# The start of a hybrid attention layer: zeros through TensorE, half of the copies on ScalarE, one chain of roots for four blocks

## The reference

```python
h = rms_norm(x, g_pre)            # x * rsqrt(mean(x*x) + eps) * g
proj = h @ w_in                   # 1024 x 7424, split in 11 parts
ya = short_gated_conv(...) * silu(a_z)
q, k = partial_rope(b_q), partial_rope(b_k)
yb = window_attention_with_sink(q, k, b_v, sink) * silu(b_z)
ym = memory_cross_attention(m_q, mk, mv) * silu(m_z)
merged = g0 * (ya @ w_up_a) + g1 * (yb @ w_up_b) + g2 * (ym @ w_up_m)
out = x + rms_norm(merged @ w_out, g_post)
```

## Time and profile before

| | us |
|---|---|
| runs | 942.90, 941.89, 942.04; median 942.04 |
| profiled execution | 942.66 |
| its span, first to last instruction | 940.8 |
| TensorE busy in the span | 915.8 (97%) |
| VectorE, ScalarE, GpSimd busy | 619.5, 422.6, 378.4 |

### The profile page before, as it was taken

How to read it: one execution, slowest core, us unless ns; L and a number is a source line. 1 busy time by engine, 2 the same in 40 slices (tenths; PEclk the granted TensorE clock), 3 DMA queues, 4 the chain that set the end, 5 groups by cost and what they waited for, 6 DMA issues and landing times. The chain is left out here.

```text
span 940.8 us, 12512 instructions
## 1 busy us (share of the span) xinstructions
PE 915.8 (97%) x4360; PEld 768.4 (82%) x4360; DVE 619.5 (66%) x1057; ACT 422.6 (45%) x802; POOL 378.4 (40%) x260
## 2 busy tenths in 40 slices
PE   5999999999999999999999999999999999999997
PEld 4788778888888888888888888888888888888885
DVE  5799966655556666656576278888896367763443
ACT  7434465444445466544462434343443553432211
POOL 2457834444444344444434744444442644300000
PEclk9999999999999999999999999999999999999999
DMA  7242656342424333624253422222222874641222
GB/s 281 85 119 82 168 175 204 103 157 101 157 101 160 110 118 107 194 95 171 100 173 132 146 67 80 84 83 81 79 78 85 320 234 146 224 156 68 90 90 89
DMA packets 81181, 124.43 MB, mean 132 GB/s; under 512 B 7008, under 2 KB 40416, under 8 KB 81120
## 3 DMA queue, kind: packets, MB, share of 16 engines
q1 hardware_dynamic: 81120, 123.65, 39.8%
HBM read 90.46 MB, written 33.55 MB: 132 GB/s over the span
## 5 line engine op out<-in xcount | busy, mean ns | idle before, releaser
L660 POOL TENSOR_TENSOR ring<-spots,ring 128x512 fp32r<-128x512 f32 x218 | 311.9, 1434 | 401.7 <-ACT ring L1063 388.9
L733 PE MATMUL pm<-hc,ring 128*128 128x512 f32 x728 | 286.7, 394 | 2.2 <-POOL ring L660 2.2
L735 PE MATMUL pm<-hc,ring 128*128 128x512 f32 x728 | 284.1, 390 | 0.0
L734 PE MATMUL pm<-hc,ring 128*128 128x512 f32 x728 | 283.7, 390 | 0.0
L1063 ACT ACTIVATE ring<-spots 128x512 fp32r<-128x512 f32 x218 | 136.6, 628 | 260.3 <-PE pm L735 183.8
L733 PEld LDWEIGHTS pm<-hc,ring 128*128 128x128 f32 x728 | 136.8, 188 | 29.3 <-issue 2.5
L735 PEld LDWEIGHTS pm<-hc,ring 128*128 128x128 f32 x728 | 136.6, 188 | 28.9
L734 PEld LDWEIGHTS pm<-hc,ring 128*128 128x128 f32 x728 | 136.8, 188 | 26.8
L1289 ACT ACTIVATE area<-area 128x1024 f32<-128x1024 f32 x24 | 25.5, 1061 | 60.6 <-DMA area<-raw_d 60.6
L1013 PE MATMUL pm<-hc,ring 128*128 128x512 f32 x128 | 49.9, 390 | 0.0
L1014 PE MATMUL pm<-hc,ring 128*128 128x512 f32 x128 | 49.8, 389 | 0.0
(11 more groups left out here) (206 smaller groups left out, 1617.6 us busy)
## 6 DMA issues: line engine op xcount, KB each, us to landing
spots<-in_w SPq DMA_DIRECT2D x116, 256.0 KB, 3.0
raw_d<-area SPq DMA_DIRECT2D x72, 256.0 KB, 2.0
area<-raw_d SPq DMA_DIRECT2D x24, 512.0 KB, 3.5
area<-in_x SPq DMA_DIRECT2D x16, 512.0 KB, 4.8
spots<-in_wup SPq DMA_DIRECT2D x24, 256.0 KB, 3.9
q_d<-area_r SPq DMA_DIRECT2D x16, 256.0 KB, 4.4
area<-raw_d SPq DMA_DIRECT2D x16, 256.0 KB, 3.2
area<-in_wmem SPq DMA_DIRECT2D x16, 256.0 KB, 2.9
```

The lines of the kernel that those rows point to most:

```text
L660: nc.gpsimd.tensor_tensor(ring[:, n % RING, 1, :], operand(n), ring[:, n % RING, 0, :].bitcast(F32), ALU.subtract).then_inc(lo_made, 1)
L733: pe.matmul(bank, hi, moving_hi(k), start=(k == 0), stop=False)
L734: pe.matmul(bank, hi, moving_lo(k), start=False, stop=False)
L735: mm = pe.matmul(bank, lo, moving_hi(k), start=False, stop=(k == HC - 1))
```

## The change

Five edits, all before or at the first Strassen pair, and one in `inv_root` that also touches the end.

1. GpSimd clears a corner of `snaps`, and TensorE multiplies it by itself 24 times (128x128) before it waits for x.
2. Blocks 4 to 7 share one chain of mean, root and reciprocal instead of two. Block 3 is scaled by ScalarE, 4 by VectorE, 5 by GpSimd, 6 and 7 by ScalarE. VectorE takes the square sum of block 4.
3. `inv_root` has four instructions instead of five.
4. ScalarE makes the full copies of chunks 8 to 15 right behind their high parts. The low part of chunk 4 goes from GpSimd to VectorE.
5. On VectorE the sums T1, T3 and T2 stand in the loop over chunks 12 to 15 (T3 and T2 came behind the first rotary tile), and T1's low parts stand ahead of `rotate(3)` and `rotate(4)`, where they stood in P6 of the first Strassen pair.

```diff
+WARM_STEPS = 24
+ROOT_GROUPS = (slice(0, 2), slice(2, 4), slice(4, NB))
+POOL_CHUNKS = (2, 6, 8, 10, 12, 14)
...
-            return sum((m % 2 == 0 and m > 0) == (sem_of is h_lo_pool) for m in range(n + 1))
+            return sum((m in POOL_CHUNKS) == (sem_of is h_lo_pool) for m in range(n + 1))
...
+            nc.gpsimd.memset(snaps[:, 0, 0:P], 0.0).then_inc(warm_made, 1)
             pool.wait_ge(xs_made, 2)
...
-            for n in range(4, 2 * KC, 2):
+            pool.wait_ge(inv_made, 2)
+            nc.gpsimd.tensor_scalar(f32(X0 + 5 * D, D), f32(X0 + 5 * D, D), st[:, 9, 5:6], None,
+                                    ALU.mult).then_inc(xs_pool, 1)
+            for n in POOL_CHUNKS[1:]:
                 low_of_h(n)
...
+            pe.wait_ge(warm_made, 1)
+            for _ in range(WARM_STEPS):
+                pe.matmul(pm[:, 1, 0:P], snaps[:, 0, 0:P], snaps[:, 0, 0:P], start=True, stop=True)
             pe.wait_ge(ident_landed, 32)
             for pair in range(2):
                 pe.wait_ge(xs_made, pair + 1)
+                if pair:
+                    pe.wait_ge(xs_act, 1)
...
+            def copy_h(n):
+
+                nc.scalar.activation(f32(H_BLOCKS[n][2], HALF), spare[n % 4], ACT.Identity,
+                                     scale=gpre[:, n % KC:n % KC + 1]).then_inc(h_copied_act, 1)
...
             high_part(0)
             high_part(1)
-            square_sum(4)
+            act.wait_ge(inv_made, 1)
+            nc.scalar.activation(f32(X0 + 3 * D, D), f32(X0 + 3 * D, D), ACT.Copy,
+                                 scale=st[:, 9, 3:4]).then_inc(xs_act, 1)
...
             for n in range(2 * KC):
                 high_of_h(n)
+                if n >= KC:
+                    copy_h(n)
                 if n == 1:
                     square_sum(5)
                 if n == 2:
+                    square_sum(6)
                     high_part(2)
+                if n == 3:
+                    square_sum(7)
                     high_part(3)
-                if n == 3:
-                    square_sum(6)
-                if n == 4:
                     roots(2)
-                    square_sum(7)
-                if n == 6:
-                    roots(3)
-                    act.wait_ge(inv_made, 1)
+                if n == 5:
+                    act.wait_ge(inv_made, 2)
                     for b in range(6, NB):
...
                 link(nc.vector.reciprocal(r, root))
-                link(nc.vector.tensor_tensor(t, r, r, ALU.mult))
+                link(nc.vector.scalar_tensor_tensor(out=t, in0=r, scalar=-0.5, in1=r, op0=ALU.mult, op1=ALU.mult))
                 link(nc.vector.tensor_tensor(t, t, var, ALU.mult))
-                link(nc.vector.tensor_scalar(t, t, -0.5, 1.5, ALU.mult, ALU.add))
-                ins = nc.vector.tensor_tensor(r, r, t, ALU.mult)
+                ins = nc.vector.scalar_tensor_tensor(out=r, in0=t, scalar=1.5, in1=r, op0=ALU.add, op1=ALU.mult)
...
-            scale_pair(0)
-            scale_pair(1)
+            variances(0)
+            inverses(0)
+            scale_x((0, 1))
+            variances(1)
+            inverses(1)
+            scale_x((2,))
+            square_sum(4)
             for n in range(2 * KC):
                 copy_h(n)
                 if n == 3:
-                    scale_pair(2)
-                if n == 5:
-                    scale_pair(3)
+                    variances(2)
+                    inverses(2)
+                if n == 4:
+                    scale_x((4,))
                 if n >= KC + HC:
-                    sum_t1(n - KC - HC)
+                    j = n - KC - HC
+                    sum_t1(j)
+                    sum_t3(j)
+                    sum_t2(j)
             swap_rows(0)
             times_cos(0)
-            for j in range(HC):
-                sum_t3(j)
-            for j in range(HC):
-                sum_t2(j)
             rotate(0)
...
             sum_s4(P_DIRECT)
+            low_of_combination(T1)
             rotate(3)
             rotate(4)
...
                     add_p6(p)
-                    if p == P_DIRECT:
-                        low_of_combination(T1)
```

More of the change, by code:

```diff
@@ L664, in low_of_h @@
                 idx, j, place = H_BLOCKS[n]
-                pool.wait_ge(h_copied, n + 1)
+                if n < KC:
+                    pool.wait_ge(h_copied, n + 1)
+                else:
+                    pool.wait_ge(h_copied_act, n - KC + 1)
                 pool.wait_ge(h_hi_made, n + 1)
@@ L756, in first_pair @@
                         if 4 <= m < 2 * KC:
-                            pe.wait_ge(h_copied, m - 3)
+                            if m - 4 < KC:
+                                pe.wait_ge(h_copied, m - 3)
+                            else:
+                                pe.wait_ge(h_copied_act, m - 3 - KC)
+                                pe.wait_ge(h_lo_dve, h_lo_count(m - 4, h_lo_dve))
                             turn_x(m)
@@ L1074, in square_sum, with roots @@
                                      accum_out=st[:, 0, b:b + 1]).then_inc(ssq_made, 1)
-            def roots(pair):
-                cols = slice(2 * pair, 2 * pair + 2)
-                act.wait_ge(var_made, pair + 1)
+            def roots(group):
+                cols = ROOT_GROUPS[group]
+                act.wait_ge(var_made, group + 1)
                 nc.scalar.activation(st[:, 2, cols], st[:, 1, cols], ACT.Sqrt).then_inc(root_made, 1)
@@ L1135, in _ @@
             high_part(7)
-            act.wait_ge(ssq_made, NB)
+            act.wait_ge(ssq_made, NB - 1)
             high_of_combination(T3)
@@ L1358, in inv_root, with square_sum, variances, inverses @@
                     ins.then_inc(done, 1)
-            def scale_pair(pair):
-                cols = slice(2 * pair, 2 * pair + 2)
-                dve.wait_ge(ssq_made, 2 * pair + 2)
+            def square_sum(b):
+                dve.wait_ge(x_landed[b], 16)
+                block, dump = f32(X0 + b * D, D), spots[:, S1:S2 + 1, :].rearrange("p n w -> p (n w)")
+                nc.vector.tensor_tensor_reduce(out=dump, in0=block, in1=block, scale=1.0, scalar=0.0, op0=ALU.mult,
+                                               op1=ALU.add, accum_out=st[:, 0, b:b + 1]).then_inc(ssq_dve, 1)
+            def variances(group):
+                cols = ROOT_GROUPS[group]
+                dve.wait_ge(ssq_made, (2, 4, 7)[group])
+                if group == 2:
+                    dve.wait_ge(ssq_dve, 1)
                 nc.vector.tensor_scalar(st[:, 1, cols], st[:, 0, cols], 1.0 / D, EPS, ALU.mult,
                                         ALU.add).then_inc(var_made, 1)
-                dve.wait_ge(var_made, pair + 1)
-                dve.wait_ge(root_made, pair + 1)
+            def inverses(group):
+                cols = ROOT_GROUPS[group]
+                dve.wait_ge(var_made, group + 1)
+                dve.wait_ge(root_made, group + 1)
                 inv_root(st[:, 1, cols], st[:, 2, cols], st[:, 9, cols], st[:, 10, cols],
[L1368 to L1373, removed]
+                         done=inv_made if group else None)
+                at_least(dve, inv_made, group)
+            def scale_x(blocks):
+                for b in blocks:
+                    ins = nc.vector.tensor_scalar(f32(X0 + b * D, D), f32(X0 + b * D, D), st[:, 9, b:b + 1], None,
+                                                  ALU.mult)
+                ins.then_inc(xs_made, 1)
             def copy_h(n):
@@ L1378, in copy_h @@
                 g = gpre[:, n % KC:n % KC + 1]
-                dve.wait_ge(h_hi_made, n + 1)
-                if n == 0 or n % 2:
+                if n < KC:
+                    dve.wait_ge(h_hi_made, n + 1)
+                elif n % 2:
+                    dve.wait_ge(h_copied_act, n - KC + 1)
+                if n not in POOL_CHUNKS:
                     nc.vector.scalar_tensor_tensor(out=hc[:, idx, 1, j, :], in0=spare[n % 4], scalar=g,
@@ L1383, in copy_h @@
                                                    op1=ALU.subtract).then_inc(h_lo_dve, 1)
-                nc.vector.tensor_scalar(f32(place, HALF), spare[n % 4], g, None, ALU.mult).then_inc(h_copied, 1)
+                if n < KC:
+                    nc.vector.tensor_scalar(f32(place, HALF), spare[n % 4], g, None, ALU.mult).then_inc(h_copied, 1)
             def sum_t1(j):
                 b11, b12 = f32(B11F + j * HALF, HALF), f32(B12F + j * HALF, HALF)
-                dve.wait_ge(h_copied, KC + j + 1)
+                dve.wait_ge(h_copied, j + 1)
+                dve.wait_ge(h_copied_act, j + 1)
                 dve.wait_ge(h_lo_pool, h_lo_count(HC, h_lo_pool))
```

12 lines of the change are left out of this document (7 added, 5 removed).

## The result

| | before | after |
|---|---|---|
| median of 22 runs each, side by side | 942.47 (941.86 to 943.99) | 944.58 (942.64 to 947.97) |
| profiled execution | 942.66 | 945.19 |
| its span | 940.8 | 943.4 |

The ratio is 1.0023 with an interval of 1.0015 to 1.0032: the change makes the kernel 0.23% slower. The forecast was 938.9 us, 3.1 faster, and the range ended at 941.8. Between the two profiled executions lie 2.53 us.

What follows compares the result with a forecast made beforehand. TensorE, busy 915.8 of 940.8 us, was taken as the bound. A first-pair lead of 2.5 us would become 2.9 at the keys, plus 0.2 at the tail: 942.04 - 3.1 = 938.9 us, range 936.3 to 941.8.

Steps and rivals of the forecast that it cites:

- What bounds the kernel: Whole kernel: TensorE is busy 915.8 of 940.8 us, so only its idle time, clock and start can be won.
- the releaser of P5: TensorE's wait of 2.16 us at P5 of pair 3: released by T1's low parts on VectorE, not GpSimd's L660.
- the sums ahead of low part 15: VectorE in the last four chunks: eight sums of 0.62 to 0.8 us replace eight copies; cost 0, bounds 0 to 2.
- the margin of 0.8: End of the first pair: low part 15 ready at about 41.7, where TensorE wants it at 42.5.
- The clock: First pair: after the zeros, products run at full clock from the start, worth 2.5 us of lead.
- My first rival: Between zeros and first product the clock falls again; lead 0.8 us, keys gain 1.3, time 940.5 us; chance 0.28.
- The lead passes through to the end: Behind `scores` no TensorE wait is over 2 us, so the keys' 2.9 us pass to the end.
- Start and roots: Kernel start: first product moves from 15.60 to about 15.0, 0.6 us of lead; shorter `inv_root` saves 0.2 at the tail.
- T1 ahead: T1's low parts before the rotations: they cost 2.6 us there, P5's 2.16 us wait goes, keys land 2.9 sooner.
- rotations later: T1's low parts delay the last rotation by 2.4 us and keys land at 122.4; time 944.2 us; chance 0.10.
- The sum: First pair's end: start 0.6 plus clock 2.5 less small waits 0.6 gives 2.5 us of lead, ending at 44.1.
- Four signs of being wrong: In the next profile: distances of 0.43 behind 15, next pair after 45.5, `scores` at or after 120, an unnamed new wait.

Runs made afterwards that it cites:

- e4: The changed kernel with T1's low parts back in P6 of the first Strassen pair; 942.97 us, ratio 1.0003 to the kernel before.
- e11: The kernel before with only T1's low parts moved ahead of the last two rotations; 943.84 us, ratio 1.0012 to the kernel before.
- e3: The changed kernel with the sums of the last two columns (j = 2 and 3) behind low part 15; 939.44 us, ratio 0.9966 to the kernel before.
- e1: The changed kernel with the sums T3 and T2 back behind the first rotary tile; 940.47 us, ratio 0.9978 to the kernel before.
- e6: The kernel before with only the memset and 24 multiplications of zeros added; 943.45 us, ratio 1.0008 to the kernel before.
- e7: e3 with T1's low parts also back in P6 of the first Strassen pair; 939.06 us, ratio 0.9963 to the kernel before.
- e9: The changed kernel with 12 more multiplications of zeros ahead of chunk 15's products; 948.06 us, ratio 1.0057 to the kernel before.
- e10: The changed kernel without zeros and with both VectorE orders (sums, T1's low parts) as before; 939.69 us, ratio 0.9965 to the kernel before.
- e12: e7 without its multiplications of zeros; 940.72 us, ratio 0.9974 to the kernel before.
- e2: The changed kernel without its 24 multiplications of zeros; 945.57 us, ratio 1.0029 to the kernel before.
- e5: e3 with 28 zeros instead of 24, and 8 and 4 more behind the two transpose groups; 940.70 us, ratio 0.9979 to the kernel before.
- e8: The kernel before with 28 zeros ahead of x and 8 and 4 behind the two transpose groups; 943.74 us, ratio 1.0015 to the kernel before.

## Why the prediction was wrong

*What bounds the kernel.* Right in its views, and the releaser of P5 was read right (e4, e11).

*The step that failed: the sums ahead of low part 15, "I take nothing, and keep 0 to 2 as bounds".* The bound went by one row, a sum of 1.11 us. It doesn't even follow from that row: nine sums stand ahead of low part 15, 0.49 more for each is 4.4 us, and the margin of 0.8 leaves 3.6, not 2. I read it as a slower rate, but it was a wait. That sum started 0.74 us after a GpSimd instruction of 1.29 (timeline of GpSimd in the kernel before, two instructions of which the first counts):

```profile
42.81 2.99 POOL L660 TENSOR_TENSOR ring<-spots,ring 128x512 fp32r<-128x512 f32 x2
```

So it waited for the rest, 0.55, and then took its own 0.55. A sum that starts right behind GpSimd's instruction waits for all of it and takes 1.6 to 1.8. The Trainium skill has this as a rule ("SBUF — State Buffer", "Who interferes with whom"): VectorE with two inputs in SBUF and GpSimd share one pair of ports by an exclusive lock, and the second one to issue blocks until the first is done. Every row here agrees (1.61 to 1.77 for such sums, 0.68 or 0.69 for the others, 1.71 and 1.80 for a GpSimd instruction that came second), and I didn't weigh it. Of the nine sums ahead of low part 15, four did: (1.61 - 0.68) x 2 + (1.77 - 0.68) + (1.76 - 0.68) = 4.0 us. Low part 15 began at 45.84 and was ready at 46.58, where I had 41.7; TensorE waited 2.67, then ran at half the clock from 48.20 for another 3.4 us, worth 1.6. e3 takes only the three last sums away from there and is 5.1 us faster. I also priced "a sum" but not what stands behind it on the engine: the rule should have been that nothing goes ahead of the last low part while TensorE's margin is 0.8 us.

*The clock.* I took 2.5 us of lead for a full clock from the first product. My first rival was right about the clock: behind the zeros TensorE idled, and the clock fell (0.52 in 14 to 16, 0.50 until 20). It had 940.5 us for that case without a loss from the sums, and e1, which is nearly that case, measured 940.47. In all seven kernels with just these 24 zeros (after, e1, e3, e4, e6, e7, e9) the first products are slow; in the two with 12 more behind the transposes they are fast. The Trainium skill ("TensorE: Matmul & The Clock Gate", Part 4) has it that transposes don't engage the full clock. Four kernels with nothing but 16 transposes ahead agree (before, e10, e11, e12: 0.43 apart at the start), and one, e2, doesn't: there the measurement says otherwise. e2 and e10 are the same program up to chunk 12, with transposes from 9.94 and 9.95 and products from 14.82 in both, so the difference isn't in what they issue; what made it the runs don't show.

*The lead passes through to the end.* I had it that behind `scores` no wait is over 2 us. In after this held (2.3 us there, 2.6 at the end), but not as a rule: e5, e8 and e9 wait 2.5 to 4.2 in the memory step, and in e2 and e9 most of the lead over after at the store (1.7 and 1.6) was gone at `scores` (0.3 and 0.5). What the table bears out is rougher. The six kernels whose store is 1.5 us or more sooner than in before are all faster, and the four whose store is 0.8 or more later are slower or the same. The size doesn't follow: e3, 1.6 sooner, gains more than e1, 2.8 sooner.

*Start and roots.* The first product came at 15.13 for 15.0. The two groups of transposes began at 9.48 and 12.89, where I had 9.5 and 12.65. GpSimd's scaling of block 5 has its row now, and took more than my upper bound of 2.4. It ends at 24.76 instead of 24.1, and no wait of TensorE is put down to it:

```profile
21.86 2.90 POOL L698 TENSOR_SCALAR area<-area,st 128x1024 f32<-128x1024 f32 x1 [0.51 <-DVE st L1384]
```

*T1 ahead.* The two low parts took 4.59 us ahead of the rotations instead of 2.6, again beside GpSimd. P5's wait went from 2.16 to 0.94, for the bank, which I had as 0 to 0.7. Its effect on the keys was small (0.3 of 48 us), so the rival "rotations later" came out near the result (944.2) by luck, with the wrong mechanism.

*The sum.* The second pair was to start at 44.1 and started at 48.20: 0.1 from the start, 2.67 from the wait, and the remaining 1.3 from the clock. At the store it is 5.2 (74.40 for 69.2), by the slow clock behind the wait less what GpSimd gave back, and the forecast (3.1 faster) and the profiled result (2.5 slower) lie 5.6 apart. Four signs of being wrong had been named, and all four came: distances of 0.43 behind 15, a second pair after 45.5, `scores` behind 120, and a wait that wasn't named.

## What to carry to other kernels

When VectorE work with two SBUF operands is moved ahead of something that the bounding engine waits for, price each instruction with the GpSimd instruction that may stand before it (here 1.7 us, not 0.68), and keep it behind the last operand that is waited for. Find the wait that is tied to another engine's chain (here a store, some 48 us ahead of the keys) and judge every gain by whether that chain starts sooner; here a lead of the bounding engine alone came back as a longer wait (e2, e9), with a slow clock behind it. Of a change of five edits, run the ones apart that touch the same engine: one line separated 0.2% slower from 0.3% faster.

## What the runs showed of the hardware

- Two-operand instructions of VectorE on SBUF and GpSimd's took turns in every stretch shown, each waiting for the other's end. VectorE's that read PSUM did not: low part 15 in e3 took 0.74 us at 41.65, in the midst of GpSimd's two (41.14 to 44.58).
- The length of one wait does not tell whether TensorE's clock falls behind it. At chunk 15, 2.67 us of idle were followed by 0.56 in after and by 1.00 in e2. At `scores`, the clock fell behind 1.80 us in e1 (0.66 in 116 to 120), 1.90 in e12, 2.07 in e5, 2.17 in after, 5.5 in e9 and 5.8 in e2 (0.50 in 120 to 124); it stayed at 1.00 behind 1.92 in before, 2.40 in e10 and 2.55 in e11. In e7 it fell at P5 (0.57 in 104 to 108, a wait of 2.2), while e10 and e12 waited as long there and kept 1.00.
- The fall behind the zeros came at different times: in after the clock column still read 1.00 over the mostly idle stretch from 8 to 14, in e3 it read 0.66 in 10 to 12 already.
